# Projecting the index key, the head weights and the gate rank as 88 columns with tokens as rows, in a three-block transformer kernel

## What is computed

```python
(qa, ka, va, iq, ik, iw, qb, kb, vb, g_low, og) = _split(proj, AB_SIZES)
iq = rope_partial(iq.reshape(bsz, s_len, IDX_HEADS, IDX_DIM), pos)     # 8 heads of 64
ik = rope_partial(ik[:, :, None, :], pos)[:, :, 0, :]                  # one key of 64
logits = jnp.einsum('bthd,bsd->bths', iqb, ik) * IDX_DIM ** -0.5
score = jnp.einsum('bths,bth->bts', jax.nn.relu(logits), iwb * IDX_HEADS ** -0.5)
gate = g_low @ w_gate_up + b_gate                                      # rank 16
```

## Time and profile before

| | |
|---|---|
| median of 3 timings | 1667.03 us (1666.4 to 1668.13) |
| profiled execution | 1665.84 us, span 1664.0 us |
| TensorE busy | 1630.5 us, 98%, 7650 matmuls |
| VectorE, ScalarE, GpSimd busy | 880.1, 603.0, 262.2 us |
| mean granted clock of TensorE | 0.992 of full |
| HBM read | 143.5 MB, 88 GB/s over the span |

### The profile page before, as it was taken

The page is one execution under the profiler, slowest core; times in us unless marked ns, Lnnn a source line. Parts: engine busy times, 40 slices in busy tenths (PEclk is TensorE's granted clock), DMA queues, the critical chain, the costliest instruction groups (busy, mean ns, idle before and its releaser), DMA issues.

```text
span 1664.0 us, 20092 instructions
## 1 busy us (share of the span) xinstructions
PE 1630.5 (98%) x7650; PEld 1324.2 (80%) x7650; DVE 880.1 (53%) x1168; ACT 603.0 (36%) x801; POOL 262.2 (16%) x288
## 2 busy tenths in 40 slices
PE   7999999999999899999999999999999999999999
PEld 7888787887777677788888888888886888888887
DVE  6334554665788776553433434467666543434343
ACT  6323332234343444432222223466765422212121
POOL 0001111023344354220111102200001210101010
PEclk9999999999999899999999999999999999999999
DMA  6222222222212121222232222222121232222222
GB/s 208 101 101 76 76 89 87 102 101 76 77 51 76 42 76 51 76 102 96 82 101 101 101 96 83 100 76 77 51 76 40 87 105 98 102 101 90 94 94 101
DMA packets 25012, 146.56 MB, mean 88 GB/s; under 512 B 3680, under 2 KB 4976, under 8 KB 8304
## 3 DMA queue, kind: packets, MB, share of 16 engines
q1 hardware_dynamic: 24944, 145.62, 25.2%
HBM read 143.52 MB, written 2.10 MB: 88 GB/s over the span
## 4 chain that ended last, share of the span: by engine, by line
PE 88%; DVE 8%; ACT 2%; issue 1%; DMA 0%; POOL 0%; SPq 0%; DVEq 0%; ACTq 0%; POOLq 0%
PE ps_G L430 27%; PE ps_G L432 26%; PE ps_G L431 26%; PE ps_ST L493 1%; PE ps_C L511 1%; DVE wide L1900 1%; DVE top L1896 1%; PE ps_AV L843 1%; PE ps_SX L698 1%; PE ps_C L528 1%; PE ps_C L843 1%; PE ps_C L616 1%; PE ps_AV L643 1%; PE ps_C L715 1%; DVE tmp L1583 0%
## 5 line engine op out<-in xcount | busy, mean ns | idle before, releaser
L430 PE MATMUL ps_G<-nh,wh 128*128 128x512 f32 x1056 | 414.7, 393 | 1.4 <-DVE wide L1693 0.8
L432 PE MATMUL ps_G<-nh,wl 128*128 128x512 f32 x1056 | 411.7, 390 | 0.0
L431 PE MATMUL ps_G<-nl,wh 128*128 128x512 f32 x1056 | 411.7, 390 | 0.0
L994 ACT ACTIVATE wh<-raw 128x2048 fp32r<-128x2048 f32 x129 | 246.2, 1909 | 322.1 <-PE ps_G L432 307.7
L430 PE MATMUL ps_G<-ch,wh 128*128 128x512 f32 x880 | 354.9, 403 | 0.0
L431 PE MATMUL ps_G<-cl,wh 128*128 128x512 f32 x880 | 345.2, 392 | 0.0
L432 PE MATMUL ps_G<-ch,wl 128*128 128x512 f32 x880 | 344.9, 392 | 0.0
L1550 DVE TENSOR_TENSOR wl<-raw,wh 128x2048 fp32r<-128x2048 f32 x114 | 263.3, 2310 | 133.0 <-ACT wh L994 129.4
L430 PEld LDWEIGHTS ps_G<-nh,wh 128*128 128x128 f32 x1056 | 198.6, 188 | 48.8 <-issue 7.5
L432 PEld LDWEIGHTS ps_G<-nh,wl 128*128 128x128 f32 x1056 | 198.4, 188 | 41.7
L431 PEld LDWEIGHTS ps_G<-nl,wh 128*128 128x128 f32 x1056 | 198.5, 188 | 40.8 <-issue 0.5
(11 more groups left out here) (312 smaller groups left out, 1681.0 us busy)
## 6 DMA issues: line engine op xcount, KB each, us to landing
raw<-wst SPq DMA_DIRECT2D x130, 1024.0 KB, 4.8
raw<-wst SPq DMA_DIRECT2D x4, 512.0 KB, 6.5
h<-xT SPq DMA_DIRECT2D x8, 256.0 KB, 6.1
outT<-h SPq DMA_DIRECT2D x8, 256.0 KB, 2.0
tabs<-rb_d SPq DMA_DIRECT2D x1, 1024.0 KB, 10.3
tabs<-tab_d SPq DMA_DIRECT2D x1, 1024.0 KB, 4.9
tabs<-tab_d SPq DMA_DIRECT2D x1, 512.0 KB, 3.9
small<-small_d SPq DMA_DIRECT2D x1, 192.0 KB, 7.9
```

Source lines behind the costliest of these rows:

```text
L430: mm(o, ah, bh, start=first, stop=False)
L431: mm(o, ah, bl, start=False, stop=False)
L432: return mm(o, al, bh, start=False, stop=last)
L994: A(wh[s][:], raw[s][:], ACT.Copy).then_inc(w_hi, 1)
```

## The change

Blocks 4 and 5 of the index stage become one product with tokens as rows. The third weight tile now holds the key (64 columns), the gate rank (16) and the head weights (8), and the rest is zero. For each of the 4 token tiles TensorE holds 128x128 of the activations stationary and moves 88 weight columns, 8 chunks x 3 terms, into one bank (C2). ScalarE scales each token's row by its norm and copies the key, twice side by side, into `fb[:, 0]`, and gate rank and head weights into `low_gate`. VectorE rotates the 16 first numbers of the key there, by a table with tokens as rows that one more DMA brings. TensorE transposes key and gate rank halfway through block 0 of the GLA stage, and ScalarE copies both out. Head weights stay by token. VectorE's residual scalings come in threes, so its split of the first GLA tile (L1550) stands behind six of them, where it stood behind four.

```diff
-          ("index", 1, 3, 6), ("gla", 2, 3, 6), ("dsa", 2, 3, 6), ("outab", 2, 2, 4),
+          ("index", 1, 3, 4), ("gla", 2, 3, 6), ("dsa", 2, 3, 6), ("outab", 2, 2, 4),
...
+        IK, GL, IW, IZ = 0, 64, 80, 88
+        keys = fb[:, 0, :].rearrange("p (t d n) -> p t d n", t=NT, d=2)
+        low_gate = PTB[:, 512:608].rearrange("p (t n) -> p t n", t=NT)
+        turn_cos = SbB[:, 512:640].rearrange("p (t d n) -> p t d n", t=NT, d=2)
+        turn_sin = SbB[:, 640:768].rearrange("p (t d n) -> p t d n", t=NT, d=2)
+        turned_by = [SbB[:, a:a + 128].rearrange("p (t d n) -> p t d n", t=NT, d=2) for a in (768, 896)]
...
-        for r in range(5):
+        for r in range(4):
             book("SX", ("perm", r))
-        book("SX", ("iw",))
+        book("C2", ("mixed",))
+        book("SX", ("keys",))
+        book("AV", ("gate_in",))
...
-            sp.dma_start(wg[32:48, :], wg_d).then_inc(tables_in, 16)
+            sp.dma_start(wg[0:16, :], wg_d).then_inc(tables_in, 16)
+            passed(sp, done["AV"], mix_use(4, "AV", 0))
+            sp.dma_start(SbB[:, 512:768], turn_d).then_inc(tables_in, 16)
...
-            for k in range(6):
+            for k in range(4):
...
+            need_tile(st, 2)
+            take(("mixed",))
+            o, s = bank_of(("mixed",)), st.slot(2)
+            for t in range(NT):
+                x = slice(t * P, (t + 1) * P)
+                for c in range(KC):
+                    ins = three(o[:, t * IZ:(t + 1) * IZ], mh[:, c, x], ml[:, c, x], wh[s][:, c, 0:IZ],
+                                wl[s][:, c, 0:IZ], c == 0, c == KC - 1)
+            ins.then_inc(done[use[("mixed",)][0]], 1)
+            perm(3, tmp[:, 3, :])
+
+            def key_turns(c):
+
+                if c != KC // 2:
+                    return
+                take(("keys",))
+                pe.wait_ge(key_set, 1)
+                for t in range(NT):
+                    ins = nc.tensor.transpose(ps["SX"][:, t * P:(t + 1) * P],
+                                              fb[:, 0, t * P:(t + 1) * P], ident)
+                ins.then_inc(done["SX"], 1)
+                take(("gate_in",))
+                settled(pe, ("mixed",))
+                for t in range(NT):
+                    ins = nc.tensor.transpose(ps["AV"][0:16, t * P:(t + 1) * P], low_gate[:, t, 0:16], ident)
+                ins.then_inc(done["AV"], 1)
...
-                    stands(pe, Step("index", 0), 5)
                     if p == 0:
-                        take(("iw",))
-                        for t in range(NT):
-                            last = nc.tensor.transpose(ps["SX"][:, t * 8:t * 8 + 8],
-                                                       wide[0:8, 15, t * P:(t + 1) * P], ident[0:8, 0:8])
-                        last.then_inc(done["SX"], 1)
+                        settled(pe, ("gate_in",))
                     take(("gate", p))
-                    pe.wait_ge(tables_in, 32)
-                    mm(ps["SX"][:], wg[32:48, p * P:(p + 1) * P], wide[32:48, 15, :],
+                    mm(ps["SX"][:], wg[0:16, p * P:(p + 1) * P], wide[0:16, 15, :],
                        start=True, stop=True).then_inc(done["SX"], 1)
...
+                        if p == k == 0:
+                            key_turns(c)
...
+                    ready(act, ("mixed",))
+                    settled(act, ("rt", 2))
+                    o = bank_of(("mixed",))
+                    for t in range(NT):
+                        z = t * IZ
+                        A(keys[:, t], o[:, z + IK:z + IK + 64].rearrange("p (d n) -> p d n", d=1).to_broadcast([P, 2, 64]),
+                          ACT.Copy, scale=rt[:, t:t + 1]).then_inc(key_raw, 1)
+                    for t in range(NT):
+                        z = t * IZ
+                        ins = A(low_gate[:, t, :], o[:, z + GL:z + IZ], ACT.Copy, scale=rt[:, t:t + 1])
+                    ins.then_inc(moved[use[("mixed",)][0]], 1)
                     act.wait_ge(rope_out, 5)
-                if p == 0:
                     split(st, 0)
+                    ready(act, ("keys",))
+                    A(wide[:, 4, :], ps["SX"][:], ACT.Copy).then_inc(moved["SX"], 1)
+                    ready(act, ("gate_in",))
+                    A(wide[0:16, 15, :], ps["AV"][0:16, :], ACT.Copy).then_inc(moved["AV"], 1)
...
-            for r in range(5):
+            pool.wait_ge(tables_in, 48)
+            for r in range(4):
                 rope_cos(r, tabI[0], tmp[:, r % 2, :])
+            pool.wait_ge(rope_c, 4)
+            pool.sem_inc(rope_c, 1)
...
-            for k in range(6):
+            for k in range(4):
...
-                dst = tmp[:, 2 + k % 2, :] if k < 5 else wide[:, 15, :]
-                moved_block(tt(dst, ready_block(st, k), r2, ALU.mult), st, k)
+                moved_block(tt(tmp[:, 2 + k % 2, :], ready_block(st, k), r2, ALU.mult), st, k)
...
-                for c in ((), (), (0, 1), (2, 3), (4, 5), (6, 7))[k]:
+                for c in ((), (), (0, 1, 2), (3, 4, 5))[k]:
                     last = stt(out=h[:, c, :], in0=h[:, c, :], scalar=par[:, G_FINAL + c:G_FINAL + c + 1],
                                in1=tmp[:, 5, :], op0=ALU.mult, op1=ALU.mult)
                 if k >= 2:
                     step(last)
-                if k == 5:
-                    applied()
                 if k:
                     rope_add(k - 1, tabI[1], tmp[:, (k - 1) % 2, :], wide[:, k - 1, :])
-            ready(dve, ("iw",))
-            moved_use(ts(iw[:].rearrange("p t n -> p (t n)"), ps["SX"][:, 0:32], 8 ** -0.5, None, ALU.mult), ("iw",))
+            split(st, 2)
+            for c in (6, 7):
+                last = stt(out=h[:, c, :], in0=h[:, c, :], scalar=par[:, G_FINAL + c:G_FINAL + c + 1],
+                           in1=tmp[:, 5, :], op0=ALU.mult, op1=ALU.mult)
+            step(last)
+            applied()
+            rope_add(3, tabI[1], tmp[:, 1, :], wide[:, 3, :])
+            dve.sem_inc(rope_out, 1)
+            dve.wait_ge(key_raw, 4)
+            by_cos, by_sin = turned_by
+            tt(by_cos, keys[:, :, :, 0:16], turn_cos, ALU.mult)
+            tt(by_sin[:, :, :, 0:8], keys[:, :, :, 8:16], turn_sin[:, :, :, 0:8], ALU.mult)
+            step(tt(by_sin[:, :, :, 8:16], keys[:, :, :, 0:8], turn_sin[:, :, :, 8:16], ALU.mult))
+            tt(keys[:, :, :, 0:16], by_cos, by_sin, ALU.add).then_inc(key_set, 1)
+            settled(dve, ("mixed",))
+            step(ts(iw[:], low_gate[:, :, 16:24], 8 ** -0.5, None, ALU.mult))
...
-    z = np.zeros((D, P), w.dtype)
-    z[:, 0:8] = w[:, IW:IW + 8]
-    z[:, 32:48] = w[:, GL:GL + 16]
-    parts += [w[:, IQ:IQ + 512], w[:, IK:IK + 64], w[:, IK:IK + 64], z]
+    parts += [w[:, IQ:IQ + 512], w[:, IK:IK + 64], w[:, GL:GL + 16], w[:, IW:IW + 8],
+              np.zeros((D, 2 * P - 88), w.dtype)]
```

More of the change, by code:

```diff
@@ L123, in step, with build @@
             self.eng.wait_ge(self.sem, self.i * self.per + (self.done + self.k))
-def build(nc, xT, wst, par_d, wg_d, rb_d, small_d, swap_d, tab_d, out):
+def build(nc, xT, wst, par_d, wg_d, rb_d, small_d, swap_d, tab_d, turn_d, out):
     with ExitStack() as ctx:
@@ L198, in build @@
         idx_acc = sem("idx_acc")
+        key_raw, key_set = sem("key_raw"), sem("key_set")
         g_log, g_scan, g_exp, g_prod, g_silu = (sem(n) for n in ("g_log", "g_scan", "g_exp", "g_prod", "g_silu"))
@@ L833, in turn_perm @@
                         if k == g == 0:
-                            pe.wait_ge(tables_in, 64)
+                            pe.wait_ge(tables_in, 80)
                         perm(rope + k, tmp[:, 2 + (rope + k) % 2, :])
@@ L1471, in _ @@
             out_squares("out1", 2)
-            pool.wait_ge(tables_in, 32)
-            for r in range(5):
+            pool.wait_ge(tables_in, 48)
+            for r in range(4):
                 rope_cos(r, tabI[0], tmp[:, r % 2, :])
+            pool.wait_ge(rope_c, 4)
+            pool.sem_inc(rope_c, 1)
             def split(st, k):
@@ L1501, in _ @@
                 split(st, 2)
-            pool.wait_ge(tables_in, 64)
+            pool.wait_ge(tables_in, 80)
             for gr in range(3):
@@ L1831, in rope_add @@
                 dve.wait_ge(rope_out, r + 1)
-            dve.wait_ge(tables_in, 32)
+            dve.wait_ge(tables_in, 48)
             st = Step("index", 0)
             r2 = fb[:, 1, :]
-            for k in range(6):
+            for k in range(4):
                 if k % 2 == 0:
@@ L2115, in attention_group @@
                     output(prev + 1)
-            dve.wait_ge(tables_in, 64)
+            dve.wait_ge(tables_in, 80)
             step(v.tensor_copy(ident_r[:], ident))
@@ L2250, in constants, with by_token @@
     earlier = np.where(j < i, 0.0, NEG).astype(np.float32)
-    return small, np.concatenate([pa, earlier], 1), np.stack([ca, sa, ci, si])
+    def by_token(a):
+        return a.T.reshape(NT, P, 1, 16).repeat(2, 2).transpose(1, 0, 2, 3).reshape(P, 8 * 16)
+    sign = np.repeat(np.array([-1.0, 1.0], np.float32), 8)[:, None]
```

(6 more changed lines are left out.)

## The result

The changed kernel takes **1671.46 us** (median of 7 runs, 1669.24 to 1673.32) where the kernel before, beside it on the chip, takes 1666.4 (median of 7, 1664.48 to 1668.13): 1.0033 times as long, 95% interval 1.0022 to 1.0044. It is slower by some 5 us. The forecast was 1672.0. The profiled execution of the changed kernel is its fastest run (1669.24 us, span 1667.4, mean granted clock 0.990); that of the kernel before took 1665.84 us.

The account below looks back on a forecast made before the run. TensorE, busy for 98% of the span, was taken to bound the kernel. Work and waits of -0.8 us and clock of +5.8 summed to +5.0: 1672.0 us against the median, range 1664.0 to 1676.5 (the forecast's own 1668 to 1675).

Parts of the forecast that it names:

- The step of 0.112: New token projection on TensorE: each of 96 matmuls takes 0.112 us, set by its weight load; 10.75 us in all.
- the expected saving is not there: Index projection: 10.9 us of removed matmuls against 10.75 us of added ones, together -0.15 us.
- The bound of 4.8 us: New projection if only columns count, 0.05 us a step; as a rival 1659.5 us, chance 0.06.
- Swap product, border, transposes, key wait: TensorE from fifth rotation into next stage: -0.86, -0.86, +0.87 and +0.2 us; with the projection's -0.15, -0.8 us.
- the 0.2: Halfway through block 0 of the next stage: TensorE waits for the rotated key, 0 to 1.6 us, taken as +0.2.
- The fall of the clock: In the new projection: thin steps bring the clock to half; with dense work and old fall, +5.8 us.
- The time into the stretch, 4.8 us: New projection: the clock falls 4.8 us in, with 43 matmuls done; range 3.2 to 8 us.
- 53 slow steps of 0.22: Rest of the new projection after the clock's fall: 53 steps of 0.22 in place of 0.112 us, +5.7 us.
- The dense tail: Dense work behind the new projection still runs slow for a while: 0 to 1.6 us, taken as +0.9.
- The old fall at 443.4: Clock fall behind the gate product in the kernel before: may go, -1.6 or 0 us, taken as -0.8.
- Full clock throughout: Rival on the new projection: the clock stays at full, -0.8 and half the old fall, 1665.4 us; chance 0.27.
- Early fall and late keys: Rival: clock falls 3.2 us in (+1.4), key late (+1.4), dense work pays more (+2.2); 1677.0 us, chance 0.07.

Follow-up runs that it names:

- the thick version: Changed kernel with the token projection moving 128 columns in place of 88, the 40 more being zeros: 1665.67 us, 0.9994 of the kernel before.
- the two-byte ones: Changed kernel with 96 more matmuls of the same shape, operands read as two-byte numbers, in front of the 96: 1678.79 us, 1.0076 of the kernel before.
- the spread one: Changed kernel with the same 96 matmuls in four pieces of 24, dense work or a swap product between: 1665.32 us, 0.9998 of the kernel before.
- the version with pairs: Changed kernel with two of four token tiles moved into the last index block, two stretches of 48 matmuls: 1672.84 us, 1.0041 of the kernel before.

## Why the prediction was right

Point by point, at full clock from the thick version, and the clock from the changed kernel itself.

- *The step of 0.112.* Right: 0.1115 measured, 0.11 at 44, 88 and 128 columns. (At 176 it is 0.12 where such matmuls stand in a row.) The projection took 10.67 us at full clock where the text had 10.75, so "the expected saving is not there" held. The bound of 4.8 us stood on a line through columns, and that line is good only for two-byte numbers.
- *Swap product, border, transposes, key wait.* Their sum with the projection was -0.8; the section shows -0.83. From the last swap product to the gate product are 7.47 us in the thick version (434.60 to 442.07); less 0.86 and 24 dense steps (5.45) 1.16 us are left for the eight transposes, where 0.87 + 0.2 stood. There was no wait in the changed kernel or in the thick one: the 0.2 was for nothing, and the transposes cost a little more than their loads. The wait is real all the same: 0.95 us of idle time appears when the projection loses 4.7 us.
- *The fall of the clock.* Right in kind, and shown by two edits that leave the work alone. The time into the stretch, 4.8 us, was a middle between 3.2 and 6.3; stretches of this width fell at 3.4, 4.6, 5.6 and 7.0, and at 4.7 behind the two-byte ones. That the middle was near is luck: one program gave 5.6 and 7.0. The text had 53 slow steps of 0.22; the profile has 36 of 0.213. Slow steps cost 3.62 us in the profiled execution (15.15 us from swap product to swap product, against 11.53) and 5.06 in the next (438.96 - 422.37 - 11.53), where 5.7 was forecast. The dense tail cost 1.17 and 1.36 (445.81 - 437.17 and 447.79 - 438.96, less 7.47), with 0.9 taken and 1.6 as the bound.
- *The old fall at 443.4.* Mis-sized. It was taken as half gone, -0.8. In none of the thirteen profiles with the change in some form does the clock fall in the 8 us behind the gate product, so the eight slow steps of 0.42 are gone and with them 1.6 us. But almost none of that is kept. The same group of index scores, of the kernel before and of the changed one, with the wait that the changed one has ahead of it:

```profile
463.08 0.92 PE L715 MATMUL ps_C<-wide 64*128 64x384 f32 x4
```

```profile
459.77 0.91 PE L753 MATMUL ps_C<-wide 64*128 64x384 f32 x2 [0.31 <-ACT sq L1249]
...
467.58 0.92 PE L753 MATMUL ps_C<-wide 64*128 64x384 f32 x4
```

  Behind the gate product that is 22.01 us before and 21.77 now: 0.24 gained. TensorE, no longer slowed, waits for ScalarE to empty the banks of the index scores (four waits in the changed kernel and in the thick version, none before). So this term was worth -0.24 there, not -0.8.
- *The sum.* -0.83, +4.79 to +6.42 and -0.24 make +3.7 to +5.4 us up to this place; the medians say +5.1. Behind it the clock falls in every version again, mostly at the same places but not for the same time: in all it is at half for 17 to 31 us in the fourteen profiles, and for 23.9 us in both that of before and that of after. In the same window the granted clock is 0.77 in the thick version and 0.89 in the spread one:

```profile
545.00:560.00 15.00, 12.58 (x52) 9.40 (x53) 13.66 (x28) 6.70 (x8) 2.46 (x3) 0.77 0.15 44
```

```profile
545.00:560.00 15.00, 12.58 (x52) 9.72 (x52) 13.66 (x25) 6.70 (x8) 3.63 (x5) 0.89 0.16 44
```

Whether the change shifts these falls or they vary by themselves stays open: there are one or two profiles of a version, and one of the kernel before. That the forecast met the median to 0.5 us owes something to errors of opposite sign: too many slow steps (+5.7 where 3.6 and 5.1 were measured) against too much gain from the old fall (-0.8 where it was -0.24) and too little for the dense tail.

- *Rivals.* "Full clock throughout" is what the kernel would have been: 1665.4 forecast, 1665.67 and 1665.32 measured with the clock held (-0.83 and -0.24 on the median of before give 1666.0). What the text said for it was read too short: the clock held at 491 to 494.6 us, but in the same profile of before it fell 3.4 us later:

```profile
498.00:501.40 3.40, 3.40 (x10) 2.62 (x8) 3.26 (x12) 0.00 (x0) 1.15 (x2) 0.50 0.26 53
```

  So that stretch was weak evidence that short matmuls keep the clock. The rule of the Trainium skill that idleness brings the throttle (TensorE: Matmul & The Clock Gate, section "The HAM clock gate (the “warmup” mystery)") doesn't describe the new projection: TensorE's busy time was 7.00 of 7.00 us before the fall. "Early fall and late keys": the early fall happens (3.4 us in the version with pairs), the late key doesn't here. Its +5.0 is also added up some 0.2 short: 14 more slow steps are +1.5, and the dense work +0.7 and +1.6.

## What to carry to other kernels

Count weight loads before columns: with four-byte operands a matmul cost 0.11 us here from 44 to 128 columns and 0.12 at 176 and 256, so turning tokens into rows to save columns saves nothing unless it saves loads too. And look at how much of each step streams: a continuous run of thin matmuls can lose the clock, and then padding with zeros, splitting the run, or merging two loads into one gives it back; the padding to 128 columns cost nothing. Do not count a fall that goes as won: behind it another engine's wait took 1.3 of the 1.6 us. Where a term is only a correction that 8 bits can carry, reading its upper two bytes in place makes its loads nearly free, if matmuls of one type stay together.

## What the runs showed of the hardware

- With a two-byte stationary operand of 128 columns a step of 88 columns takes 0.039 us, and 0.04 where it is read with a stride of four bytes; a rounded four-byte one sets a step of 0.11 at full clock and 0.213 at half.
- Streaming more made the kernel faster: 128 columns in place of 88 took 1665.67 us in place of 1671.4.
- TensorE fully busy with 44- or 88-column steps lost the clock after 3.2 to 7.0 us, at different times in two executions of one program; 96 two-byte steps of 88 columns did not in the 3.75 us that they took, nor did 96 four-byte ones of 128 columns in 10.7 us, or 64 of 88 and 176 mixed in 7.1.
- A four-byte matmul of 176 columns alternating with a two-byte one of 88 takes 0.21 us a pair; in groups of eight, eight pairs took 1.26 us (5.03 / 4), 0.157 a pair.
